# Projection tiles 4 to 27 in pairs by seven block products, in a hybrid streaming layer on one core

## The reference

```python
u = x @ w_in
...
full = jnp.concatenate([shift_buf.astype(u.dtype), u], axis=1)
us = u + (full[:, :-1] - u) * mu
r, k, v, w_low, a_low, g_low = _split(us, (RWKV_DIM, RWKV_DIM, RWKV_DIM, RWKV_W_RANK, RWKV_A_RANK, RWKV_G_RANK))
```

## Time and profile before

| | |
|---|---|
| median of 3 runs | 1505.3 us (1504.83 to 1505.84) |
| span of the profiled execution | 1502.1 us (its own time beside the span is not given) |
| TensorE busy | 1457.5 us, 97% |
| VectorE busy | 647.1 us, 43% |
| ScalarE busy | 390.4 us, 26% |
| GpSimd busy | 116.8 us, 8% |
| mean granted TensorE clock | 0.996 of full speed |

### The profile page before, as it was taken

How to read it: one execution, slowest core, us unless ns; L and a number is a source line. 1 busy time by engine, 2 the same in 40 slices (tenths; PEclk the granted TensorE clock), 3 DMA queues, 4 the chain that set the end, 5 groups by cost and what they waited for, 6 DMA issues and landing times.

```text
span 1502.1 us, 31068 instructions
## 1 busy us (share of the span) xinstructions
PE 1457.5 (97%) x13071; PEld 1011.2 (67%) x13071; DVE 647.1 (43%) x1227; ACT 390.4 (26%) x874; POOL 116.8 (8%) x107
## 2 busy tenths in 40 slices
PE   7999999999999999999999999999999999999995
PEld 6776667677776777767766765766666767675751
DVE  5223778875644677734541114622211112121228
ACT  2112444442322554435431011111111111111111
POOL 3000113121010000000000000000000001000000
PEclk9999999999999999999999999999999999999998
DMA  7778375563344544565577538689999999999985
GB/s 243 168 174 181 101 214 166 132 203 97 103 130 147 138 112 116 178 180 163 135 231 263 157 100 359 251 337 399 417 423 430 428 426 429 426 428 429 427 342 211
DMA packets 157017, 375.27 MB, mean 250 GB/s; under 512 B 101708, under 2 KB 110300, under 8 KB 139216
## 3 DMA queue, kind: packets, MB, share of 16 engines
q1 hardware_dynamic: 123712, 341.35, 63.9%
q10 hardware_dynamic: 26592, 15.49, 3.5%
q0 software_dynamic: 6576, 16.48, 3.2%
HBM read 327.14 MB, written 51.95 MB: 252 GB/s over the span
## 4 chain that ended last, share of the span: by engine, by line
PE 82%; DVE 7%; DMA 4%; ACT 2%; DVEq 2%; issue 1%; SPq 1%; ACTq 1%; POOLq 0%
PE PS L576 27%; PE PS L1069 14%; PE PS L919 8%; PE PS L1036 7%; PE PS L1088 6%; PE PS L624 4%; PE PS L1041 2%; PE PS L957 2%; DVE region L1492 2%; DVE region L1499 2%; PE PS L632 1%; ACT L1172 1%; PE PS L1052 1%; PE PS L1077 1%; PE PS L817 1%
## 5 line engine op out<-in xcount | busy, mean ns | idle before, releaser
L576 PE MATMUL PS<-h0T,region 128*128 128x320 f32 x1808 | 510.2, 437 | 1.0 <-issue 0.8
L576 PEld LDWEIGHTS PS<-h0T,region 128*128 128x128 f32 x1808 | 336.8, 190 | 144.6 <-issue 12.2
L1172 ACT ACTIVATE region<-PS 128x9 f32<-128x9 f32 (+6 forms) x407 | 148.5, 383 | 681.9 <-PE PS L576 311.8
L1069 PE MATMUL PS<-region 128*64 128x512 f32 x1024 | 228.8, 592 | 0.0
L1069 PEld LDWEIGHTS PS<-region 128*64 128x64 f32 x1024 | 124.5, 137 | 92.2 <-issue 31.9
L1492 DVE TENSOR_TENSOR region<-region 128x256 f32<-128x256 f32 (+10 forms) x210 | 127.0, 624 | 96.8 <-ACTq L1218 76.2
L919 PE MATMUL PS<-region 128*128 128x320 f32 x512 | 138.6, 433 | 1.3 <-DMA region<-wo 1.2
L919 PEld LDWEIGHTS PS<-region 128*128 128x128 f32 x512 | 97.0, 190 | 42.5 <-issue 1.7
L1172 ACT ACT_TABLE_LOAD x80 | 102.6, 1283 | 73.1 <-DMA region<-projected 56.7
L1088 PE MATMUL PS<-region,history 128*64 128x512 f32 x512 | 119.7, 596 | 1.0 <-ACTq L1454 0.7
L1172 ACT ACTIVATE region<-region 128x256 f32<-128x256 f32 (+8 forms) x160 | 81.2, 531 | 147.9 <-DMA region<-projected 37.0
(11 more groups left out here) (210 smaller groups left out, 1163.8 us busy)
## 6 DMA issues: line engine op xcount, KB each, us to landing
region<-moe_w SPq DMA_DIRECT2D x64, 2048.0 KB, 17.4
region<-moe_w SPq DMA_DIRECT2D x64, 1024.0 KB, 15.0
region<-w_in SPq DMA_DIRECT2D x115, 512.0 KB, 5.6
region<-wo SPq DMA_DIRECT2D x32, 512.0 KB, 3.6
projected<-region ACTq DMA_DIRECT2D x65, 167.5 KB, 3.9
expert_rows<-region SPq DMA_DIRECT2D x20, 512.0 KB, 7.2
region<-expert_rows SPq DMA_DIRECT2D x5, 2048.0 KB, 14.4
region<-projected SPq DMA_DIRECT2D x10, 768.0 KB, 6.3
```

The costliest lines, as they stand in the source:

```text
L576: last = mm(PS[:, 6 + i % 2, 0:NTOK], WR[:, i, k, :], H0T[:, k, :], start=(k == 0), stop=(k == KT - 1))
L1069: last = mm(PS[tiles(i), 2, :], XE[:, k, tiles(i)], W13[r][i][:, k * 512:k * 512 + 512], start=(k == 0), stop=(k == KT - 1))
L1172: return nc.scalar.activation(out, in_, f, **kw)
```

## The change

Tiles 4 to 27 are made in 12 pairs. A pair's weights are two tiles by two halves of the features (blocks A11, A12 and A21, A22, each 512 by 128) and the tokens are two halves of the features by two halves of each chunk (32 columns each, 160 in all). The four results, of 128 by 160 each, come from seven block products of four matmul steps each, where before there were eight. For that sums and differences are needed: of tokens, once (`TSUM`, four operations of 640 columns), of weights, for each pair (`WSUM`, four operations of 512 columns), and of products. ScalarE copies four partial sums of each pair out of PSUM (`keep`) and TensorE waits for each copy before it adds onto, or overwrites, the bank; VectorE makes the four results (`quads`).

There are eight weight slots for the pairs (`WR` and `EARLY`). The weights of tiles 4 to 7 are loaded at the start, ahead of `LNB` and the small weights. Stores of tiles 4 to 26 are issued by SyncE (`paired_out`). ScalarE makes `(1 - mu) * u` into `CV` and VectorE adds `mu` times the previous token in one operation (`paired_shift`). The order of tiles in the pairs is permuted (`head_row`): the low-rank tiles come before those of v, and `first_rows` fetches the v rows last. `LNB` lies elsewhere, and GpSimd drains after each operation. VectorE makes the token sums and the weight sums of pairs 0 and 1 before its shifts of tiles 0 to 3.

```diff
+            def paired(p):
+                ring, a = pair_weights(p)
+                for k in range(2):
+                    n = RING + 2 * p + k
+                    if p > 1:
+                        sp.wait_ge(sem("tile_done"), n - 2 * RING + 1)
+                    landed = f"early_in_or_rows_in{a + k}" if ring is EARLY else f"weights_in{a + k}"
+                    sp.dma_start(ring[:, a + k, :, :], io['w_in'][head_row(n), :, :, :]).then_inc(sem(landed), 16)
+            for p in range(2):
+                paired(p)
             for k in range(2):
                 sp.dma_start(LNB[:, k, :], io['lnv'][k:k + 1, :].to_broadcast([128, D])).then_inc(sem("ln_in"), 16)
...
+                pe.wait_ge(sem("quads_out"), pair + 1)
+                product(X, lambda k: ring[:, a, k, :], lambda k: H0H[:, k, 0], True)
+                product(Z, lambda k: ring[:, b, KH + k, :], lambda k: TSUM[:, 3, k], True)
+                pe.wait_ge(sem("weights_summed"), pair + 1)
+                pe.wait_ge(sem("quad_kept"), pair * 4 + 1)
+                product(X, lambda k: WSUM[u][:, 1, k], lambda k: TSUM[:, 1, k], False)
+                pe.wait_ge(sem("quad_kept"), pair * 4 + 2)
+                product(Z, lambda k: ring[:, a, KH + k, :], lambda k: H0H[:, KH + k, 0], True)
+                product(W, lambda k: WSUM[u][:, 0, k], lambda k: TSUM[:, 0, k], True, True)
+                pe.wait_ge(sem("quad_kept"), pair * 4 + 3)
+                product(X, lambda k: WSUM[u][:, 2, k], lambda k: TSUM[:, 2, k], False)
+                pe.wait_ge(sem("quad_kept"), pair * 4 + 4)
+                product(W, lambda k: WSUM[u][:, 3, k], lambda k: H0H[:, KH + k, 1], False)
...
+            pe.wait_ge(sem("token_sums"), 1)
+            with pe.Fori(0, PAIRS // 4) as m:
+                for p in range(4):
+                    project_pair(m, p)
...
+            for p in range(PAIRS):
+                keep(p, 1, 0, X)
+                keep(p, 2, 2, Z)
+                if p > 0:
+                    paired_edges(p - 1)
+                keep(p, 3, 1, X)
+                keep(p, 5, 3, W)
+            paired_edges(PAIRS - 1)
...
+            for p in range(2):
+                weight_sums(p)
+            for n in range(RING):
                 shift(n)
+            for p in range(PAIRS):
+                quads(p)
+                if p + 2 < PAIRS:
+                    weight_sums(p + 2)
+                for n in range(RING + 2 * p, min(RING + 2 * p + 2, T_MISC)):
+                    paired_shift(n)
```

More of the change, by code:

```diff
@@ L315, in first_rows, with stored @@
+            def stored(e):
                 for i in range(RING):
                     sp.wait_ge(sem(f"store_done{i}"), 16 * ((e - 1 - i) // RING + 2))
[L317 to L330, removed]
+            def first_rows(a, e, landed):
+                sp.dma_start(USS[:, 0, a:e], ut[a:e, :, 0, HIST:CW].rearrange("t p w -> p t w")).then_inc(sem(landed), 16)
+            for p in range(2, 4):
+                paired(p)
+            for p in range(PAIRS):
+                if p + 4 < PAIRS:
+                    paired(p + 4)
+                if p + 2 >= PAIRS:
+                    for n in range(RING + 2 * (p + 2), RING + 2 * (p + 2) + 2):
+                        weights(n // RING, n % RING)
+                if p > 0:
+                    paired_out(p - 1)
+                if p == 5:
+                    stored(10)
+                    first_rows(0, 10, "rw_us0")
+                if p == 9:
+                    stored(18)
+                    first_rows(10, 16, "rw_us0")
+                    first_rows(24, 26, "rw_us0")
@@ L581, in project, with project_pair, product @@
                 project_part(m, i, range(KT))
+            def project_pair(m, p):
+                pair = m * 4 + p
+                u = p % 2
+                ring, a = pair_weights(p)
+                b = a + 1
+                X, Z, W = (quad_sum(3 * u + x) for x in range(3))
+                def product(out, lhs, rhs, start, freed=False):
+                    for k in range(KH):
+                        last = mm(out, lhs(k), rhs(k), start=start and k == 0, stop=k == KH - 1, skip_group_check=True)
+                        if freed and k < 2:
+                            last.then_inc(sem("tile_done"), 1)
+                    last.then_inc(sem("quad"), 1)
+                for i in (a, b):
+                    if p < 2:
+                        pe.wait_ge(sem(f"early_in_or_rows_in{i}"), m * 16 + 16)
+                    else:
+                        pe.wait_ge(sem(f"weights_in{i}"), m * 16 + 80)
+                pe.wait_ge(sem("quads_out"), pair + 1)
[11 more added lines that the diff above has]
+                product(W, lambda k: WSUM[u][:, 3, k], lambda k: H0H[:, KH + k, 1], False)
             pe.wait_ge(sem("ident_in"), 32)
@@ L1226, in move, with keep, edges, paired_edges @@
                 act.dma_start(ut[n, :, :, :], STG[:, i, :, :]).then_inc(sem(f"store_done{i}"), 16)
-            for n in range(PRE):
-                move(n // RING, n % RING)
+            def keep(p, made, x, region):
+                act.wait_ge(sem("quad"), 7 * p + made)
+                a_(kept(p % 2, x), region, ACT.Copy)
+                act.drain().then_inc(sem("quad_kept"), 1)
+            def edges(n):
+                i = n % RING
+                act.wait_ge(sem(f"store_done{i}"), (n // RING + 1) * 16)
+                src = STG[:, i, :, HIST:CW]
+                a_(STG[:, i, 1:NPC, 0:HIST], src[:, 0:NPC - 1, L - HIST:L], ACT.Copy)
+                a_(STG[:, i, 0:NCH:NPC, 0:HIST], HISTS[:, head_row(n), :, :], ACT.Copy)
+                if n >= T_XBC:
+                    k = n - T_XBC
+                    a_(CVO[:, :, k, :], src[:, NPC - 1:NCH, L - HIST:L], ACT.Copy)
+                    a_(CV[:, i], src, ACT.Identity, scale=VEC[:, V_CW + 72 + k:V_CW + 73 + k], bias=VEC[:, V_CB + k:V_CB + k + 1])
+                elif n < T_MISC:
+                    row = head_row(n)
+                    a_(SHO[:, :, row], src[:, NPC - 1:NCH, L - 1], ACT.Copy)
+                    a_(CV[:, i], src, ACT.Copy, scale=OMU[:, row:row + 1])
+            def paired_edges(p):
+                act.wait_ge(sem("quads_out"), p + 3)
+                for n in (RING + 2 * p, RING + 2 * p + 1):
+                    edges(n)
+                act.drain().then_inc(sem("tile_moved"), 2)
+            for n in range(RING):
+                move(n // RING, n % RING)
+            for p in range(PAIRS):
+                X, Z, W = (quad_sum(3 * (p % 2) + x) for x in range(3))
+                keep(p, 1, 0, X)
+                keep(p, 2, 2, Z)
+                if p > 0:
+                    paired_edges(p - 1)
+                keep(p, 3, 1, X)
+                keep(p, 5, 3, W)
+            paired_edges(PAIRS - 1)
             meet(act, 1)
@@ L1577, in shift, with quads @@
                 dve.drain().then_inc(sem("tile_mixed"), 1)
-            for n in range(T_MISC):
-                shift(n)
+            def quads(p):
+                u, a, b = p % 2, 2 * (p % 2), 2 * (p % 2) + 1
+                X, Z, W = (quad_sum(3 * u + x) for x in range(3))
+                dve.wait_ge(sem("quad"), 7 * p + 4)
+                dve.wait_ge(sem("quad_kept"), 4 * p + 1)
+                tt(quad_out(a, 0), kept(u, 0), Z, add)
+                dve.wait_ge(sem("quad"), 7 * p + 6)
+                dve.wait_ge(sem("quad_kept"), 4 * p + 4)
+                for j in range(2):
+                    tt(quad_out(b, j), kept(u, 2 + j), X, add)
+                dve.wait_ge(sem("quad"), 7 * p + 7)
+                tt(quad_out(a, 1), kept(u, 1), W, add)
+                dve.drain().then_inc(sem("quads_out"), 1)
@@ new lines, in _, with weight_sums @@
+            flat2 = lambda x: x.rearrange("p a b -> p (a b)")
+            def weight_sums(p):
+                u = p % 2
+                ring, a = pair_weights(p)
+                b = a + 1
+                S1, S2, S3, S4 = (flat2(WSUM[u][:, x]) for x in range(4))
+                A11, A12, A21, A22 = (flat2(ring[:, i, k * KH:k * KH + KH, :]) for i in (a, b) for k in range(2))
+                for i in (a, b):
+                    if ring is EARLY:
+                        dve.wait_ge(sem(f"early_in_or_rows_in{i}"), p // 4 * 16 + 16)
+                    else:
+                        dve.wait_ge(sem(f"weights_in{i}"), p // 4 * 16 + 80)
+                if p > 1:
+                    dve.wait_ge(sem("quad"), 7 * p - 7)
+                tt(S1, A21, A22, add)
+                tt(S3, A11, A21, sub)
+                dve.drain()
+                tt(S2, S1, A11, sub)
+                dve.drain()
+                tt(S4, A12, S2, sub)
+                dve.drain().then_inc(sem("weights_summed"), 1)
@@ new lines, in paired_shift @@
+            def paired_shift(n):
+                i, row = n % RING, head_row(n)
+                dve.wait_ge(sem("tile_moved"), n + 3)
+                stt(CV[:, i], STG[:, i, :, HIST - 1:CW - 1], VEC[:, V_MU + row:V_MU + row + 1], CV[:, i], mul, add)
```

(15 more changed lines are left out.)

93 lines of the change are left out of this document (70 added, 23 removed).

## The result

The changed kernel takes 1515.1 us (median of 4 runs, 1512.87 to 1515.76), the kernel before 1505.07 us. The ratio is 1.0074, interval 1.0058 to 1.0091: slower by some 10 us, where 1512.7 (+7.4) was forecast. The profiled execution has a span of 1513.9 us against 1502.1, +11.8.

What follows compares the result with a forecast made beforehand. TensorE alone was taken to set the pace. +14.8 + 2.0 + 1.1 - 12.0 + 1.55 = +7.4 us took the span from 1502.1 to 1509.5, and 3.2 us carried over gave 1512.7; range 1500 to 1519.

Steps and rivals of the forecast that it cites:

- The products: TensorE's twelve pairs: 56 matmuls of 160 columns at 136 ns, 7.62 us a pair instead of 8.62; -12.0 us.
- the 125 ns of the expert stage: Pace of 128-column matmuls there, used as upper bound: 156 ns per 160-column product, 8.75 us a pair.
- The waits inside a pair: ScalarE's copies and VectorE's sums in each pair finish in time for TensorE; 0 taken, 0 to 0.3 us a pair.
- The start: Before tile 3, VectorE's added work and six GpSimd operations delay the first shift, so TensorE stands; +14.8 us.
- The clock: After TensorE's gap, tile 3 starts at 1.2 GHz; +2.0 us, bounds 0 to 4.3.
- Pair 0's first copy: Pair 0's third product waits for the copy of X behind tile 3's move, shift and store; +1.1 us.
- The end of the stage: Tile 28 waits until the edges of tiles 26 and 27 are made; +1.55 us, bounds 0 to 2.5.
- the 0.32 us at 33.89: In the kernel before, tile 4's weight load waited 0.32 us for ScalarE; read as TensorE already feeling GpSimd's turns.

Runs made afterwards that it cites:

- e_late: The changed kernel with GpSimd's six operations held back, one for every second pair; 1501.5 us, ratio 0.9990 to the kernel before.
- e_three: The changed kernel with three of GpSimd's six operations left in place and three held back; 1507.5 us, ratio 1.0023 to the kernel before.
- e_order: The changed kernel with VectorE's order altered: shifts 0 and 1, weight sums of pair 0, shifts 2 and 3, weight sums of pair 1; 1507.3 us.
- e_lnb: The changed kernel with the layer norm rows loaded ahead of the four early weight tiles; 1513.9 us, ratio 1.0062 to the kernel before.
- e_end: The changed kernel with GpSimd held back, VectorE's shifts first, and tiles 28 and 29 not waiting for edges of tiles 26 and 27; 1500.3 us.
- e_warm: The changed kernel with 27 added products of 320 columns, results unused, on TensorE between tiles 2 and 3; median 1515.0 us, ratio 1.0088.
- b_late: The kernel before the change with GpSimd's six operations held back, one each after the shifts of tiles 4 to 9; 1504.0 us, ratio 1.0011.
- e_store: The changed kernel with GpSimd held back, VectorE's shifts first, and tile 3's store issued after pair 0's first two copies; 1494.05 us, ratio 0.9950.

## Why the prediction was right

Step by step, for the start of tile 28 in the two traces (147.53 - 137.77 = 9.76 us late):

- The products: -12.0 forecast, -12.1 measured. (8.62 - 7.61) x 12. The new load hides under 160 columns; the 125 ns of the expert stage was no guide.
- The waits inside a pair: 0 forecast, none shown.
- The start: +14.8 forecast, 14.9 measured, the idle 14.71 us and some 0.2 of the last matmul's tail. Its parts stand too: the rows landed at 23.48 us (23.4), all six operations were in front, 11.6 us were lost on the VectorE operations (12.0), and one more in front costs 1.8 to 2.1 us by `e_late`, `e_three` and the changed kernel.
- The clock: +2.0 forecast, +3.1 measured (7.58 - 4.47). This term was undersized: I took the middle of 0 to 4.3, and the clock came back only near the end of the tile. That a short gap would leave the clock at 1.00 was wrong as well, in `e_late`'s expectation. The price does not go by the length of the gap: gaps of 3.10, 8.99, 9.25, 14.71 and 14.81 us (`e_late`, `e_order`, `e_three`, the changed kernel, `e_lnb`) cost 3.1, 2.1, 1.7, 3.1 and 3.0 us. It is half of the time that the clock stays low after TensorE goes on (6.1, 4.3, 3.3, 6.2 and 5.9 us), and that does not follow the gap.
- Pair 0's first copy: +1.1 forecast; 1.10 idle.
- The end of the stage: +1.55 forecast, 1.74 - 0.25 = 1.5 measured. `e_end` shows more than was said: the RWKV stage behind needs the same ScalarE work, so this term can't be had back by dropping TensorE's wait.
- Not in the sum: +1.07 us before tile 2. It is in the first 16 matmuls of 128 columns. Timeline, first the kernel before, then the changed one:

```profile
13.54 2.81 PE L588 MATMUL PS<-h0T,region 128*128 128x128 f32 x16 [0.23 <-ACTq L1195]
```

```profile
13.47 3.78 PE L692 MATMUL PS<-h0T,region 128*128 128x128 f32 x16 [0.24 <-ACTq L1302]
```

The same matmuls after the same wait, and nothing in the change touches them; `e_late` and `e_three` have tile 2 at 25.29 and 25.04, the kernel before at 25.30, and `e_order` at 26.29. So it is not the change's but the run's. By its pace (at first two matmuls start every 0.43 us, 215 ns each, twice the 106 of the earlier trace rows) it looks like a later rise of the clock; that is argued, not shown, since the granted clock reads 1.00 there.

The sum of the measured terms is -12.1 + 14.9 + 3.1 + 1.3 (1.10 and the tail) + 1.5 + 1.07 = 9.8. The last 2.0 us of the span's 11.8 come after tile 28 and were in no term. In the RWKV stage TensorE stops for 1.49 us amid 32 matmuls that follow without a break in the kernel before. Timelines, first the kernel before, then the changed one:

```profile
268.00 1.15 PE L632 MATMUL PS<-region 64*64 64x64 f32 x32 [0.19 <-PE PS L632]
```

```profile
277.38 0.47 PE L737 MATMUL PS<-region 64*64 64x64 f32 x9 [0.19 <-PE PS L737]
279.35 0.91 PE L737 MATMUL PS<-region 64*64 64x64 f32 x23 [1.49 <-issue]
280.19 4.11 PE L647 MATMUL PS<-h0T,region 128*128 128x320 f32 x8
```

This stop, 1.3 to 2.2 us, is in every trace of a kernel with pairs but that of `e_warm`, and in neither trace of the kernel without them. The releaser is "issue", so what TensorE waits for the traces don't say, and it was not tried. Behind it the clock falls: the 8 matmuls of L647 take 4.11 us instead of 2.42, and the window of 276 to 284 us has a mean clock of 0.79:

```profile
276.00:284.00 8.00, 6.32 (x98) 4.55 (x93) 7.03 (x7) 5.80 (x11) 0.00 (x0) 0.79 0.95 219
```

A mean of 0.79 over 8 us is 0.21 x 8 / 0.5 = 3.4 us at the lower level, a price of 1.7 us. Another such dip lies on L1127, 8.8 us for 16 matmuls where the kernel before has 7.1; it begins at about 970 us, behind a wait of 1.04 us. The kernel before has no such dip between 147 and 1400 us. Such short dips are in eight of the twelve traces, `b_late`'s among them, and each begins within 2.1 us of the end of a stop of 1.0 to 3.1 us. `e_store` has the same stops and no dip, so a stop is not enough, and what decides is open. From the start of tile 28 to the end of the span it is 1364.3 us in the kernel before, 1365.0 in `b_late`, 1366.4 in the changed kernel, and 1363.4 to 1367.5 in the experiments with pairs where tile 28 still waits: the 2.0 us lie within what single traces differ by.

The forecast of the time came nearer than that of the span. The median was taken 3.2 us above the span, as in the kernel before; in the changed kernel it is 1.2 above. So the span came out 4.4 us over the forecast and the median 2.4: 2.0 us of the closeness are luck.

One reading of the trace was too much. I took the 0.32 us at 33.89 as TensorE already paying. It is idle time of the weight load; the matmuls of tile 4 started on the beat of 4.3 us, and `b_late` took it away and gained nothing.

## What to carry to other kernels

Before new work goes in front of an operation that frees another engine's buffer, list what shares a port or a queue with it at that moment: twelve operations and a small one, 10.4 us in `e_late`, took 22.0 because six operations of an idle engine were let in between, and the same six cost nothing when each was released where VectorE had time. A faster inner loop is worth its whole gain only if the way into it stays covered; here the pairs' 12 us were there from the first run. Holding GpSimd back, VectorE's other order and one store moved turned 10 us slower into 7.6 us faster. And a gap on TensorE can have a second price that its length does not tell: 3.1 us idle cost 3.1 us more at the lower clock, as much as 14.7 did, and 9.25 cost 1.7.

## What the runs showed of the hardware that was not expected

- A one-input VectorE operation is blocked as well: the `tensor_scalar` of 26 columns took 2.13 us beside GpSimd and 0.18 in `e_late`. The forecast had counted only operations with two SBUF inputs and was saved by the small difference. The Trainium skill (SBUF — State Buffer, Who interferes with whom) says that `tensor_scalar` can enter a mode that takes two ports and then contends with GpSimd. The trace agrees with that, 2.13 against 0.18 us; in which mode this operation ran no run here shows.
- The clock falls within a gap of 3.1 us in `e_late`, 2.4 us after TensorE's last matmul, while in the changed kernel it held for 3.8 us. How long TensorE may stand is not to be read from one gap, and short dips come even behind a stop of 1.04 us (the changed kernel near 970 us).
- A matmul of 160 columns with its own 128x128 load takes 7.61 us / 56 = 136 ns, 2.6 ns over the 133.3 ns of 160 columns at 2 cycles each; the 320-column one takes 269 ns, 2.7 ns over its 266.7.
